# A two-layer hybrid decoder trunk: tokens loaded as columns, bias rows laid out by query in memory

## The reference

```python
h = jnp.concatenate([meta, x], axis=1)
for layer in range(DEPTH):
    nw = norm_w[layer]
    f = swiglu(rms_norm(h, nw[0]), ffn_w_gate[layer, 0], ffn_w_up[layer, 0], ffn_w_down[layer, 0])
    h = h + 0.5 * rms_norm(f, nw[1])
    hn = rms_norm(h, nw[2])
    mix = even_mixer(hn, ...) if layer % 2 == 0 else odd_mixer(hn, ...)
    h = h + rms_norm(mix, nw[3])
    f = swiglu(rms_norm(h, nw[4]), ffn_w_gate[layer, 1], ffn_w_up[layer, 1], ffn_w_down[layer, 1])
    h = h + 0.5 * rms_norm(f, nw[5])
return h[:, N_META:]
# in the even mixer: scores + table[t5_bucket(query - key)] per head
```

## Time and profile before

| | us |
|---|---|
| median of 3 runs (2060.25 to 2063.73) | 2063.29 |
| profiled execution | 2064.58 |
| its span | 2062.5 |
| TensorE busy | 2037.2 |
| VectorE busy | 1381.8 |
| ScalarE busy | 1020.9 |
| GpSimd busy | 102.6 |

### The profile page before, as it was taken

The page is one execution under the profiler, slowest core; times in us unless marked ns, Lnnn a source line. Parts: engine busy times, 40 slices in busy tenths (PEclk is TensorE's granted clock), DMA queues, the critical chain, the costliest instruction groups (busy, mean ns, idle before and its releaser), DMA issues.

```text
span 2062.5 us, 38826 instructions
## 1 busy us (share of the span) xinstructions
PE 2037.2 (99%) x16054; PEld 1960.5 (95%) x16054; DVE 1381.8 (67%) x2042; ACT 1020.9 (50%) x1751; POOL 102.6 (5%) x97
## 2 busy tenths in 40 slices
PE   8999999999999999999999999999999999999998
PEld 7999999998999999999999999999998789999887
DVE  6999831667485399988228998822663449998723
ACT  5655632446535465557225555622453456555612
POOL 0000000100052200000000000010000020000000
PEclk9999999999999999999999999999999999999999
DMA  4333332321110133333313233331322122333332
GB/s 137 95 103 103 104 127 77 88 73 52 42 32 12 52 103 97 109 103 106 113 50 101 87 109 103 108 108 52 96 81 68 42 70 95 103 108 112 109 97 76
DMA packets 107539, 180.64 MB, mean 88 GB/s; under 512 B 7593, under 2 KB 73424, under 8 KB 107374
## 3 DMA queue, kind: packets, MB, share of 16 engines
q1 hardware_dynamic: 106016, 175.30, 27.3%
q0 software_dynamic: 1024, 2.86, 0.5%
q10 hardware_dynamic: 334, 0.14, 0.0%
HBM read 176.16 MB, written 2.12 MB: 86 GB/s over the span
## 4 chain that ended last, share of the span: by engine, by line
PE 95%; DVE 3%; ACT 1%; issue 0%; DMA 0%; POOL 0%; DVEq 0%; ACTq 0%
PE psum L1276 35%; PE psum L702 31%; PE psum L714 13%; PE psum L928 5%; PE psum L3161 1%; PE psum L3220 1%; DVE w_hl L564 1%; PE psum L2622 1%; PE psum L3719 1%; PE psum L2634 0%; PE psum L3735 0%; PE psum L3730 0%; DVE acts L1991 0%; PE psum L805 0%; PE psum L781 0%
## 5 line engine op out<-in xcount | busy, mean ns | idle before, releaser
L1276 PE MATMUL psum<-seven_x,w_hl 128*128 128x264 f32 (+1 forms) x3456 | 438.3, 283 | 0.0
L564 DVE TENSOR_TENSOR w_hl<-stage,w_hl 128x1024 fp32r<-128x1024 f32 (+1 forms) x166 | 220.7, 1331 | 308.9 <-ACT w_hl L557 308.6
L1276 PEld LDWEIGHTS psum<-seven_x,w_hl 128*128 128x128 f32 x3456 | 424.9, 188 | 0.0
L702 PE MATMUL psum<-x_hl,w_hl 128*128 128x264 f32 (+1 forms) x2736 | 368.3, 294 | 1.7 <-DVE w_hl L564 1.3
L702 PEld LDWEIGHTS psum<-x_hl,w_hl 128*128 128x128 f32 x2736 | 348.7, 190 | 14.2 <-issue 5.5
L1276 PE MATMUL psum<-x_hl,w_hl 128*128 128x264 f32 (+1 forms) x2592 | 338.2, 284 | 0.0
L1276 PEld LDWEIGHTS psum<-x_hl,w_hl 128*128 128x128 f32 x2592 | 324.5, 188 | 0.0
L557 ACT ACTIVATE w_hl<-stage 128x1024 fp32r<-128x1024 f32 (+1 forms) x166 | 188.9, 1139 | 213.9 <-PE psum L702 71.5
L702 PE MATMUL psum<-acts,w_hl 128*128 128x264 f32 x2376 | 289.0, 284 | 0.0
L702 PEld LDWEIGHTS psum<-acts,w_hl 128*128 128x128 f32 x2376 | 288.7, 188 | 0.0
L714 PE MATMUL psum<-x_hl,w_hl 128*128 128x264 f32 (+1 forms) x1728 | 219.2, 286 | 0.6 <-DVE w_hl L564 0.3
(11 more groups left out here) (401 smaller groups left out, 2187.9 us busy)
## 6 DMA issues: line engine op xcount, KB each, us to landing
stage<-ffn_w_down SPq DMA_DIRECT2D x48, 704.0 KB, 4.0
stage<-ffn_w_gate SPq DMA_DIRECT2D x52, 512.0 KB, 3.5
stage<-ffn_w_up SPq DMA_DIRECT2D x52, 512.0 KB, 3.6
x_raw<-ffn_w_gate SPq DMA_DIRECT2D x32, 512.0 KB, 4.2
x_raw<-ffn_w_up SPq DMA_DIRECT2D x32, 512.0 KB, 4.3
stage<-odd_w_in SPq DMA_DIRECT2D x24, 512.0 KB, 3.6
stage<-even_w_in SPq DMA_DIRECT2D x22, 512.0 KB, 3.6
stage<-ffn_w_down_rows SPq DMA_DIRECT2D x22, 512.0 KB, 3.4
```

Of the source, the lines that this page charges most:

```text
L564: dve.tensor_tensor(weights(core.w_hl[:, slot.ring, 1, :], *kind), weights(core.stage[:, slot.stage, :], *kind), weights(core.w_hl[:, slot ...
L702: op = pe.matmul(out, lhs, moving[:, moved, kt, t0:t0 + n], start=first and part + moved == 0, stop=last and part == 1)
L1276: op = pe.matmul(k.psum[:, bank, 0:w], k.w_hl[:, slot.ring, side, at:at + P], moving(moved, kt), start=start and kt + side + moved == 0, s ...
```

## The change

The host now also hands over the tokens as columns (`tokens`, [128, 8, 528], meta tokens first) and all channel vectors as columns (`channel_cols`, [128, 151]). SyncE loads the first gate weights, then two pieces of two channel tiles each straight into `h`, then the up weights, then the two other pieces. ScalarE's queue loads only the norm columns and the other vector columns; the identity goes to GpSimd's queue. All transposes of the opening go. TensorE multiplies ones by ones 16 times before it waits for the first weights. Slot 0 runs over four tiles, then come the table products, slot 1 over four tiles, then each piece for both slots. ScalarE and VectorE work by pieces: high halves and squares, low halves, with the weight splits in between; the additions of squares are four instead of three.

The bias by distance is copied in memory into one block a query: GpSimd issues 16 transfers, one after each of the first 16 groups of seven. The reads for the mixer then step one block less one element from partition to partition, which gives the right order of queries, straight into the buffers that the scores read. The flips, their copies and their waits go.

```diff
+TOKEN_PIECES = ((0, 1), (2, 3), (4, 5), (6, 7))
+WARM = 16
+BIAS_TILE = 16
+BIAS_COPIES = 16
-CONST_LOADS = 11
-SCALAR_LOADS = 6
+CONST_LOADS = 8
+SCALAR_LOADS = 2
...
 def sync_program(core, sp, a):
-    load_tokens(core, sp, a, 0)
-    sp.dma_start(core.rows_meta[:, :], a["meta_tokens"]).then_inc(core.tok_in, 16)
...
+def load_tokens(core, sp, a, piece):
+    first, last = TOKEN_PIECES[piece][0], TOKEN_PIECES[piece][-1]
+    sp.dma_start(core.h[:, first:last + 1, :], a["tokens"][:, first:last + 1, :])\
+      .then_inc(core.tokens_in[piece], 16)
...
             sp.dma_start(group_stage(core, n, side, slot), w[n])\
                 .then_inc(core.w_landed[slot.stage], 16)
+            if phase is core.phases[0] and n == 0:
+                load_tokens(core, sp, a, 2 * side)
+                load_tokens(core, sp, a, 2 * side + 1)
...
+    pe.wait_ge(k.consts_set, 1)
+    for _ in range(WARM):
+        pe.matmul(k.psum[:, 4, 0:P], k.ones[:], k.ones[:], start=True, stop=True)
+    run(slots[0], 0)
+    run(slots[0], 1)
     pe.wait_ge(k.consts_set, 5)
     pe.wait_ge(k.consts_in, 16 * (CONST_LOADS - SCALAR_LOADS))
-    pe.wait_ge(k.vectors_in, 16 * (SCALAR_LOADS - 2))
-    pe.transpose(k.psum[:, 7, 2 * P:2 * P + VEC_ROWS], k.rows_vec[0:VEC_ROWS, :], k.ident[0:VEC_ROWS, 0:VEC_ROWS])
     pe.matmul(k.psum[0:QH, 6, 0:512], k.table[:], k.bucket_hot[:, 0:512], start=True, stop=True)
...
-    for slot in slots:
-        run(slot, DT - 2)
-        run(slot, DT - 1)
+    run(slots[1], 0)
+    run(slots[1], 1)
+    for piece in (2, 3):
+        for slot in slots:
+            run(slot, piece)
...
-                if slot.local == INPUT_SLOTS and kt == DT - 2:
+                if slot.local == INPUT_SLOTS and kt == DT - 4:
                     token_sum(k, pe, phase.before)
...
+    def piece(i):
+        act.wait_ge(k.tokens_in[i], 16)
+        for kt in TOKEN_PIECES[i]:
+            col = first.before.pre_col + kt
+            act.activation(k.x_hl[:, 0, kt, :], k.h[:, kt, :], ACT.Copy, scale=k.norm_cols[:, col:col + 1])\
+               .then_inc(k.x_hi, 1)
+        for kt in TOKEN_PIECES[i]:
+            act.activation(k.in_squares[:, kt, :], k.h[:, kt, :], ACT.Square).then_inc(k.sq_made, 1)
...
+    high(0)
+    act.wait_ge(k.norms_in, 16)
+    act.wait_ge(k.vectors_in, 16)
+    piece(0)
+    piece(1)
+    high(1)
+    piece(2)
+    piece(3)
+    high(2)
     act.wait_ge(k.cols_flip, 1)
...
     root(k, act, norm)
-    act.wait_ge(k.bias_stored, 16)
...
+    if phase is k.phases[0] and n == BIAS_TILE:
+        dve.wait_ge(k.bias_stored, 16)
...
+    low(0)
+    dve.wait_ge(k.norms_in, 16)
+    dve.wait_ge(k.vectors_in, 16)
+    piece(0)
+    piece(1)
+    low(1)
+    dve.wait_ge(k.sq_made, DT // 2)
+    add_squares(0, 2, 2)
+    piece(2)
+    piece(3)
+    low(2)
     dve.wait_ge(k.sq_made, DT)
...
+    add_squares(4, 6, 2)
+    dve.wait_ge(k.sq_added, 2)
+    add_squares(0, 4, 2)
+    dve.wait_ge(k.sq_added, 3)
+    add_squares(0, 1, 1)
...
+def bias_copies(core, pool, a, phase):
...
+    k = core
+    scratch, one = a["bias_scratch"], QH * V_ALL
+    pool.wait_ge(k.bias_stored, 16)
+    for i in range(BIAS_COPIES):
+        first, last = (P - 1) * i // BIAS_COPIES + 1, (P - 1) * (i + 1) // BIAS_COPIES + 1
+        pool.wait_ge(k.act_full, phase.seven0 + i + 1)
+        pool.dma_start(scratch[first:last].rearrange("p h v -> p (h v)"),
+                       bass.AP(scratch.tensor, 0, [[0, last - first], [1, one]])).then_inc(k.bias_stored, 16)
...
-        return bass.AP(tensor, first, [[1, rows], [V_ALL, QH], [1, n]])
+        return bass.AP(tensor, first + rows - 1, [[QH * V_ALL - 1, rows], [V_ALL, QH], [1, n]])
...
-        pe.wait_ge(e.rows_in, 80)
-        for j in range(BIAS_FLIPS):
-            if j >= len(FLIP_BANKS):
-                pe.wait_ge(e.bias_set, j - len(FLIP_BANKS) + 1)
...
-        pe.wait_ge(e.bias_set, BIAS_FLIPS)
         pe.wait_ge(e.v_rows_set, 3)
...
     if s == FLIPS_AT:
-        for j in range(BIAS_FLIPS):
...
-        dve.wait_ge(e.bias_set, BIAS_FLIPS)
+        dve.wait_ge(e.rows_in, 64)
         dve.memset(e.gates[:], 1.0).then_inc(e.gates_clear, 1)
```

More of the change, by code:

```diff
@@ L233, in count @@
             before["added"] += phase.early if self.split else DT - 1
-        if not self.split:
-            before["h"] += 2 * DT
         if self.pre_col is not None:
@@ L239, in count @@
                 before["sq"] += DT
-                before["added"] += 3
+                before["added"] += 4
         if self.split:
@@ L391, in __init__ @@
         self.acts_raw = self.at("acts_raw", [P, FT, TOK], low)
+        self.bias_row = self.at("bias_row", [QH, V_ALL], low + BIAS_TILE * tile)
         self.gates_raw = self.at("gates_raw", [P, SEVEN_TILE, TOK], self.arena)
@@ L982, in tensor_input, with run @@
     slots = [Slot(phase, 0, u) for u in range(INPUT_SLOTS)]
[L984 to L1001, removed]
+    def run(slot, piece):
+        slot.out_pair = slot.pair
+        if piece == 0:
             pe.wait_ge(k.w_lo, slot.count())
-        pe.wait_ge(k.x_lo, kt + 1)
-        slot.out_pair = slot.pair
-        op = products(k, pe, phase, slot, kt, kt, k.x_hl, kt == 0, kt == DT - 1)
+        for kt in TOKEN_PIECES[piece]:
+            pe.wait_ge(k.x_lo, kt + 1)
+            op = products(k, pe, phase, slot, kt, kt, k.x_hl, kt == 0, kt == DT - 1)
         if kt == DT - 1:
             op.then_inc(k.slot_used, 1)
[L1009 to L1021, removed]
+    pe.wait_ge(k.consts_set, 1)
[3 more added lines that the diff above has]
+    run(slots[0], 1)
     pe.wait_ge(k.consts_set, 5)
     pe.wait_ge(k.consts_in, 16 * (CONST_LOADS - SCALAR_LOADS))
-    pe.wait_ge(k.vectors_in, 16 * (SCALAR_LOADS - 2))
-    pe.transpose(k.psum[:, 7, 2 * P:2 * P + VEC_ROWS], k.rows_vec[0:VEC_ROWS, :], k.ident[0:VEC_ROWS, 0:VEC_ROWS])
     pe.matmul(k.psum[0:QH, 6, 0:512], k.table[:], k.bucket_hot[:, 0:512], start=True, stop=True)
@@ L1306, in token_sum @@
 def token_sum(core, pe, norm):
-    pe.wait_ge(core.sq_added, 3)
-    pe.wait_ge(core.cols_ready, 4)
+    pe.wait_ge(core.sq_added, 4)
+    pe.wait_ge(core.cols_ready, 2)
     for b, (t0, w) in enumerate(halves(norm.cols)):
@@ L1375, in scalar_input, with high @@
     first = k.phases[0]
-    act.wait_ge(k.cols_flip, 1)
[L1377 to L1399, removed]
+    def piece(i):
[6 more added lines that the diff above has]
+            act.activation(k.in_squares[:, kt, :], k.h[:, kt, :], ACT.Square).then_inc(k.sq_made, 1)
+    def high(u):
+        split_hi(k, act, Slot(first, 0, u), (DT, P))
+    high(0)
[7 more added lines that the diff above has]
+    high(2)
+    act.wait_ge(k.cols_flip, 1)
     act.activation(k.bias_row[0:QH, 0:512], k.psum[0:QH, 6, 0:512], ACT.Copy).then_inc(k.cols_ready, 1)
@@ L1787, in scalar_program @@
     k = core
[L1788 to L1791, removed]
+    norms, vectors = const_rows(k, a)[0:SCALAR_LOADS]
+    act.dma_start(*norms).then_inc(k.norms_in, 16)
+    act.dma_start(*vectors).then_inc(k.vectors_in, 16)
     scalar_input(k, act)
@@ L2238, in vector_input @@
     first = k.phases[0]
[L2239 to L2252, removed]
@@ L2253, in vector_input, with piece @@
-    dve.wait_ge(k.sq_made, DT)
[L2254 to L2257, removed]
-        out = k.sq_sum[:, :].unsqueeze(1) if tiles == 1 else total
-        dve.tensor_tensor(out, total, k.in_squares[:, tiles:2 * tiles, :], ALU.add).then_inc(k.sq_added, 1)
+    def piece(i):
+        dve.wait_ge(k.tokens_in[i], 16)
+        for kt in TOKEN_PIECES[i]:
+            col = first.before.pre_col + kt
+            dve.wait_ge(k.x_hi, kt + 1)
+            dve.scalar_tensor_tensor(k.x_hl[:, 1, kt, :], k.h[:, kt, :], k.norm_cols[:, col:col + 1],
+                                     k.x_hl[:, 0, kt, :].bitcast(F32), ALU.mult, ALU.subtract).then_inc(k.x_lo, 1)
@@ new lines, in low, with add_squares @@
+    def low(u):
+        split_lo(k, dve, Slot(first, 0, u), (DT, P))
+    def add_squares(first, second, tiles):
+        total = k.in_squares[:, first:first + tiles, :]
+        out = k.sq_sum[:, :].unsqueeze(1) if tiles == 1 else total
+        dve.tensor_tensor(out, total, k.in_squares[:, second:second + tiles, :], ALU.add).then_inc(k.sq_added, 1)
+    low(0)
[5 more added lines that the diff above has]
+    dve.wait_ge(k.sq_made, DT // 2)
@@ L2336, in gpsimd_program @@
                 gpsimd_split(k, pool, step)
+        elif kind == "dense" and step is k.phases[0]:
+            bias_copies(k, pool, a, step)
         elif kind == "dense" and step.kind == "rows":
@@ L2343, in gpsimd_program @@
             odd_gpsimd(k, pool, step, a)
-    pool.wait_ge(k.bias_stored, 16)
+    pool.wait_ge(k.bias_stored, 16 * (BIAS_COPIES + 1))
     pool.wait_ge(k.weight_in, 16)
@@ L2411, in __init__ @@
         self.squares = at("conv_squares", [P, DH, TOK], a + Z_TILE * tile)
-        rows = a + Z_TILE * tile
-        self.bias_rows = at("bias_rows", [P, QH, BANDS], rows)
```

(19 more changed lines are left out.)

70 lines of the change are left out of this document (7 added, 63 removed).

## The result

| | before | after |
|---|---|---|
| median, us (5 runs each) | 2063.29 (2060.25 to 2064.52) | 2051.95 (2048.01 to 2054.01) |
| span of the profiled execution, us | 2062.5 | 2048.0 |

The ratio is 0.9943, with an interval of 0.9929 to 0.9956: 11.8 us faster, give or take 2.8. The forecast was 2050.7, 12.6 us faster; the medians differ by 11.3.

What follows compares the result with a forecast made beforehand. TensorE, busy 2037.2 of 2062.5 us, was taken to bound the kernel. Opening 8.9 plus mixer 3.7 gave 12.6 us, with copies at nothing: median 2063.3 to 2050.7, 80% range 2046.0 to 2057.0.

Steps and rivals of the forecast that it cites:

- The opening, 8.9 us: Start of the kernel: without transposes and norm-row wait, the first two slots end at 23.75 us instead of 32.6.
- The products of ones: Ahead of the first weights: 16 products cost nothing under the token wait and give full pace from the first product.
- rival 1: Opening: half pace up to 19 us despite the ones; opening gain only 4.9 us, time 2054.7; chance 0.15.
- The mixer, 3.7 us: Mixer: without flips, the first score product moves from 427.17 to about 423.5, next waiting on ScalarE's copy of turned values.
- The copies, nothing: First-stage groups: 16 bias copies of 0.18 MB cost nothing, with 5.6 us of slack for weight loads.
- Rival 5: First-stage groups: copies hold the DMA engines, weights come late in 16 groups, kernel slower than before, 2073 at 7 us later; chance 0.04.
- rival 3: Mixer: two falls of the granted clock, put at 3.1 us, may go (2047.6) or new ones come; chance, falls gone, 0.17.
- Transfers one behind another: Opening: six loads run in sequence at 3.5 us each, opening gain 6.3 us, time 2053.3; chance 0.05.

Runs made afterwards that it cites:

- the run of the mixer alone: Kernel before, with its old opening, given the changed mixer and the 16 bias copies in the first stage: 2057.99 us, ratio 0.9984.
- eight copies: Changed kernel with each of the 16 bias copies followed by seven more of the same size to memory nobody reads: 2052.4 us, ratio 0.9955.
- the small loads late: Changed kernel with GpSimd's identity load and three loads of single values for 128 partitions waiting for the second token piece: 2049.55 us.

## Why the prediction was right

*The opening, 8.9 us.* Measured 8.93 in the pair of profiles. The steps: first product at 8.9 (8.70), slot 1 at 14.6 (14.85), third slot at 23.75 (23.8). The mechanism was right; that the numbers agree to 0.2 us is partly luck. The terms were off in ways that cancelled: two high halves took 1.36 us where 1.2 was taken, the vector columns landed at 6.8 (I took 7.5 for the start; they, not piece 0, were last), piece 1 at 10.1 for 9.6, the up weights at 12.5 for 11.4, and the last piece at 15.0 for 14.0. The late up weights cost little, because ScalarE came to them at 12.48 and would not have come before 12.3 in the forecast either. And the pair itself was a good one: the opening of before reached the groups of seven at 68.73 and 67.15 in its two profiles, that of after at 58.97 to 59.84 in its four with the ones, so the gain is 7.3 to 9.8 us by landings alone.

*The products of ones.* Full pace from the first product, as taken. But rival 1 was mis-sized three times. Half pace takes 1.32 us a tile, not 1.7 (six products 0.22 apart): the 1.69 of rows 2 is one tile by itself with its last product's end in it. It lasted 4.3 us from the first product, to 12.6, where the rival kept it up to 19 us because it had ended there before; before, the first products had come over 4 us later and had transposes between them. And the forecast laid tile behind tile at half pace without asking what TensorE would wait for anyhow. Rival 1, priced at 4.0 us over the main case, comes to 0.2 to 0.9; the run without ones has the groups of seven at 59.56.

*The mixer, 3.7 us.* 3.71, the step from 427.17 to "3.7 earlier" and the next late thing (ScalarE's value copies) both as named. The same 3.7 stands in the run of the mixer alone.

*The copies, nothing.* The stage's length is unchanged to 0.01 us. Rival 5 was rightly placed: with eight copies the loads come to the edge of the slack and the stage grows by 3.05 us. Its price beyond that edge, each late microsecond one of the stage, was not tested.

*The clock in the mixer.* Two falls were put at 3.1 us; with and without them the mixer takes 253.40 and 250.27. That they might come and go was rival 3, and it is what the profile shows beyond 12.6 us. The ten profiles of this study have 0 to 3 falls, so 0 to 4.7 us, and the clock goes with the spread of one and the same kernel. The mean granted clock of each of the five runs of after is on record: 0.999 at 2048.01 us, 0.998 at 2049.73 and 2051.95, 0.997 at 2052.47, 0.996 at 2054.01. A mean lower by 0.003 takes 6.2 us of clock out of 2050, and the first and last of these runs are 6.0 apart. The 17 runs of the kernel before beside the first experiments part the same way: 0.999 or 1.000 up to 2061.39 us, 0.997 or 0.998 from 2062.04 on. Where in a run the clock fell is known only for the profiled ones.

*Transfers one behind another.* Didn't happen: all four token pieces and both weight loads were in flight together, at about 400 GB/s where the small loads left them alone. The Trainium skill advises batching transfers to 1 MiB and more ("DMA: Bandwidth & Descriptors", section Bandwidth). Pieces of half that lost nothing by it that the rows show: with the small loads late, pieces of 0.5 MB in flight together moved at 347 to 427 GB/s from 4 to 12 us.

Open: what makes the clock fall in some executions and not in others. Its places are the same few (about 416, 481, 515 to 526, 543 to 560), but no run here changed what TensorE does there.

## What to carry to other kernels

Lay out the opening as a timetable for each engine, with landings from the byte curve of a similar start, and ask of each stall what else TensorE would be waiting for at that moment: half pace, or a saved transfer, is worth only what stands out beyond the next wait. Small loads of a few bytes to each of 128 partitions can go behind the large ones that the first products need: here that brought the up weights 1.3 us earlier or more, and slot 1 by 0.4. Don't let the first work wait for something that it doesn't read: by the estimate above, the one for the vector columns was worth more than the order of the work behind it. And when a data layout can be bought with idle DMA time during a compute-bound stage, as the bias rows were here, check the slack of the loads beside it from issue, landing and first read.

## What was not expected of the hardware

Three loads of 2 to 4 KB each, spread over 128 partitions, with the 64 KB identity, took the rate from 411 to 79 GB/s for some 4 us; with them later the rate stayed at 347 to 427, and at 324 to 427 in the two other profiles with that order. The runs don't separate the four loads.

Without the ones, half pace lasted 4.3 and 4.2 us from the first product of weights (19 and 18 products 0.22 us apart, then 0.12). The 16 products of ones, of which all but the pace is fixed, took 5.26 to 6.73 us in different executions, so the doubling falls at different moments: 3.0 us after their start in the profile with eight copies (0.21 us from record to record, then 0.11), 6.0 us in that of after, where only the last five of 32 records ran at full pace. The first products of weights, 0.9 us behind them, were at full pace.
